# A routed expert loop: the gather with the selection as stationary operand, reading x in place

## The reference, cut to what matters

```
xn = rms_norm(x, norm2_g)                       # 384 x 1024
lg = xn @ rg_w + rg_b ; le = xn @ re_w + re_b   # 4 groups, 32 experts
grp = argmax(lg) ; two best experts in the group, softmax weights -> combine
for e in range(32):
    hdn = silu(xn @ w_gate[e]) * (xn @ w_up[e])   # 1024 -> 512, twice
    out = out + combine[:, e] * (hdn @ w_down[e]) # 512 -> 1024
x = x + out
```

## Time and profile before

| | |
|---|---|
| runs | 946.94, 952.38, 952.4 us |
| the profiled execution's own time | 949.38 us |
| its span, first to last instruction | 947.6 us |
| mean granted TensorE clock | 0.949 |
| TensorE busy | 820.5 us (87%) |
| VectorE, ScalarE, GpSimd busy | 432.2, 312.7, 269.2 us |
| bytes moved | 249.96 MB, mean 264 GB/s |
| first item's gate and up begin | 399.25 us |
| last item's Silu begins | 927.88 us |

### The profile page before, as it was taken

How to read it: one execution, slowest core, us unless ns; L and a number is a source line. 1 busy time by engine, 2 the same in 40 slices (tenths; PEclk the granted TensorE clock), 3 DMA queues, 4 the chain that set the end, 5 groups by cost and what they waited for, 6 DMA issues and landing times.

```text
span 947.6 us, 25723 instructions
## 1 busy us (share of the span) xinstructions
PE 820.5 (87%) x10726; PEld 659.0 (70%) x10727; DVE 432.2 (46%) x1128; ACT 312.7 (33%) x526; POOL 269.2 (28%) x135
## 2 busy tenths in 40 slices
PE   4999999999999999598887767868898889889884
PEld 4999999999999987366555544545666556566663
DVE  3076797899840614533233313223333333334343
ACT  5333875543377226522111111111221112122123
POOL 4755899884858851200000000000000000000000
PEclk9999999999999998799899999889999999999997
DMA  7724334254333326557999999999877999997601
GB/s 242 225 96 133 115 109 152 102 158 145 119 131 118 104 75 257 232 239 285 421 423 423 422 421 423 422 423 422 367 302 313 423 422 422 421 423 292 266 0 67
DMA packets 53170, 249.96 MB, mean 264 GB/s; under 512 B 6599, under 2 KB 6599, under 8 KB 28561
## 3 DMA queue, kind: packets, MB, share of 16 engines
q1 hardware_dynamic: 49184, 244.86, 65.4%
q10 hardware_dynamic: 3953, 4.67, 1.6%
HBM read 246.76 MB, written 2.75 MB: 263 GB/s over the span
## 4 chain that ended last, share of the span: by engine, by line
PE 51%; DVE 22%; DMA 15%; issue 7%; ACT 3%; DVEq 1%; POOL 0%; SPq 0%
PE bank L1240 22%; PE bank L1381 16%; DMA ring<-in_exp_w_up 14%; DVE bank L932 6%; PE bank L1333 4%; PE bank L1238 3%; PE bank L1367 3%; DVE cva L1131 2%; DVE back_to L1159 2%; DVE cva L1155 2%; DVE cvb L1095 1%; DVE y_lo L1168 1%; DMA raw<-in_w_in 1%; DVE ua L994 1%; DVE cvb L1099 1%
## 5 line engine op out<-in xcount | busy, mean ns | idle before, releaser
L1381 PE MATMUL bank<-ring,cvb 128*32 128x256 f32 x2816 | 194.1, 433 | 87.3 <-issue 43.6
L1381 PEld LDWEIGHTS bank<-ring,cvb 128*32 128x32 f32 x2816 | 117.5, 123 | 146.8 <-issue 118.5
L504 POOL TENSOR_TENSOR w_lo<-raw,w_hi 128x2048 fp32r<-128x2048 f32 x40 | 184.9, 4625 | 75.1 <-ACT w_hi L631 75.1
L1149 DVE SCALAR_TENSOR_TENSOR cvb<-bank,slot_coef,cvb 64x256 f32<-64x256 f32 x44 | 21.5, 489 | 289.5 <-ACT cvb L817 289.5
L1240 PE MATMUL bank<-x_hi,w_hi 128*128 128x384 f32 x448 | 150.8, 337 | 0.9 <-POOL w_lo L504 0.6
L1240 PE MATMUL bank<-x_hi,w_lo 128*128 128x384 f32 x448 | 149.7, 334 | 0.0
L1240 PE MATMUL bank<-x_lo,w_hi 128*128 128x384 f32 x448 | 149.7, 334 | 0.0
L932 DVE SCALAR_TENSOR_TENSOR bank<-ub,vec,bank 128x256 f32<-128x256 f32 (+1 forms) x416 | 137.3, 421 | 0.0
L1333 PEld LDWEIGHTS bank<-cvb,ua 128*128 128x128 bf16 x2184 | 79.8, 96 | 50.5 <-issue 38.6
L631 ACT ACTIVATE w_hi<-raw 128x2048 fp32r<-128x2048 f32 x40 | 76.7, 1919 | 83.5 <-PE bank L1240 71.2
L817 ACT ACTIVATE cvb<-bank 64x256 f32<-64x256 f32 x44 | 16.6, 376 | 249.3 <-PE bank L1381 249.3
(11 more groups left out here) (205 smaller groups left out, 1003.5 us busy)
## 6 DMA issues: line engine op xcount, KB each, us to landing
ring<-in_exp_w_gate SPq DMA_DIRECT2D x64, 1024.0 KB, 14.9
ring<-in_exp_w_up SPq DMA_DIRECT2D x64, 1024.0 KB, 16.9
ring<-in_exp_w_down SPq DMA_DIRECT2D x64, 1024.0 KB, 17.9
raw<-in_w_in SPq DMA_DIRECT2D x28, 1024.0 KB, 5.2
raw<-in_w_out_a SPq DMA_DIRECT2D x4, 1024.0 KB, 5.1
raw<-in_w_out_b SPq DMA_DIRECT2D x4, 1024.0 KB, 5.0
raw<-in_w_o SPq DMA_DIRECT2D x4, 1024.0 KB, 5.0
out<-n_tok ACTq DMA_DIRECT2D x3, 512.0 KB, 2.7
```

The costliest lines, as they stand in the source:

```text
L504: pool.tensor_tensor(w_lo[u % NW][:, :, :], raw[u % NW][:, :, :], w_hi[u % NW][:, :, :].bitcast(F32), ALU.subtract).then_inc(lo_ready, 1)
L1149: dve.scalar_tensor_tensor(hid, GU[2 * T:4 * T, :], slot_coef[2 * T:4 * T, 0:1], sig, ALU.mult, ALU.mult)\
L1381: last = pe.matmul(GU[q * T:(q + 1) * T, :], xe[:, k, :], wide(slots[q // 2])[:, k, q % 2 * QE:(q % 2 + 1) * QE], start=(k == 0), stop=(k ...
```

## The change

The gather turns round: `pick` (128 x 32, fp32) is stationary and x moves, 256 columns at a time, read from `x_tok` in place with a step of four floats between columns, so that the rows come out in the order of `by_row`. Four column groups of the array take four different quarters of the row, three token tiles are summed: 12 fp32 matmuls for an item, into `G` (32 slots x 4 blocks on the partitions, 256 columns) in bank 0. ScalarE copies `G` to `rows_of_x`, TensorE transposes it in two pieces into `XT` (the other half of bank 0), and VectorE scales that by `norm2_by_row` into `xe`. The rows are not normalised: the factor of each token (`rstd2`) goes into the slots' coefficients, and the Silu takes it as its scale.

The normalised copies, their three parts and the diagonals are gone, with ScalarE's, GpSimd's and VectorE's work for them. The slot numbers, factors and coefficients are transposed once (`values`, `turned`) and spread by matmuls whose stationary operand is a column of the identity repeated. `Y` lies in bank 0, gate and up in bank 1. The second turn of `combine` comes behind the transposes, the third between the two halves of down; the wait for `y_ready` stands before the gather, the wait for the next `xe` before down. The bounds of a pair's items come by one load of three numbers, and the table holds 33 numbers for 65.

```diff
-    for a, b in zip(range(aux("pos"), len(AUX)), (0, 1, 2, 3, 2, 3)):
+    for a, b in zip(range(aux("pos"), len(AUX)), (0, 1, 1, 2, 1, 2, 1, 2)):
...
-        XE = bank[0][:, 0:KB * T]
+        G = bank[0][:, 0:QE]
+        XT = bank[0][:, QE:2 * QE]
+        Y = bank[0][:, 0:QE]
+        GU = bank[1][:, 0:QE]
         HT = bank[1][:, 0:HK * T]
-        Y = bank[1][:, 0:QE]
-        GU = bank[1][:, 0:QE]
...
             pool.memset(back_to[:].bitcast(F32), 0.0).then_inc(back_ready, 1)
-
-            for i in range(NT):
-                pool.wait_ge(part_ready[0], i + 1)
-                pool.wait_ge(normed, NT + i + 1)
-                pool.tensor_tensor(n_tok[:, i, :], n_tok[:, i, :], parts[0][:, i, :], ALU.subtract)\
-                    .then_inc(rest_ready, 1)
-            for i in range(NT - 1):
-                pool.wait_ge(part_ready[1], i + 1)
-                pool.tensor_tensor(parts[2][:, i, :], n_tok[:, i, :], parts[1][:, i, :], ALU.subtract)\
-                    .then_inc(part_ready[2], 1)
...
-            act.wait_ge(rstd_ready, 1)
-            for i in range(NT):
-                for dst, done in ((n_tok, normed), (parts[0], part_ready[0])):
-                    act.activation(dst[:, i, :].rearrange("p (h j q) -> p h j q", h=2, j=RJ), by_row(x_tok[:, i, :]),
-                                   ACT.Copy, scale=small[:, 32 + i:33 + i]).then_inc(done, 1)
...
+            def copy_rows(n):
+
+                act.wait_ge(gathered, n)
+                act.activation(rows_of_x[:, :], G, ACT.Copy).then_inc(rows_ready, 1)
...
             def item(i):
                 act.wait_ge(gate_up_done, i + 1)
 
-                act.activation(sig, GU[0:2 * T, :], ACT.Silu).then_inc(sig_ready, 1)
+                act.wait_ge(slot_coef_ready, i + 1)
+                act.activation(sig, GU[0:2 * T, :], ACT.Silu, scale=slot_coef[0:2 * T, 0:1]).then_inc(sig_ready, 1)
+                copy_rows(i + 2)
...
             def take_gathered(n):
 
-                dve.wait_ge(gathered, n)
-                dve.tensor_tensor(xe, XE.rearrange("p (k t) -> p k t", k=KB),
-                                  norm2_by_row[:, :].unsqueeze(2).to_broadcast([P, KB, T]), ALU.mult)\
-                   .then_inc(xe_ready, 1)
+                dve.wait_ge(x_turned, n)
+                dve.tensor_tensor(xe[:, :, :].rearrange("p (q b) t -> p q b t", b=2),
+                                  XT.rearrange("p (b q t) -> p q b t", b=2, q=TILES),
+                                  norm2_by_row[:, :].rearrange("p (q b) -> p q b", b=2).unsqueeze(3)
+                                  .to_broadcast([P, TILES, 2, T]), ALU.mult).then_inc(xe_ready, 1)
...
-            def gather(blocks):
-
-                for k in blocks:
-                    for c in range(3):
-                        for i in range(NT):
-                            last = pe.matmul(XE[:, k * T:(k + 1) * T], parts[c][:, i, k * P:(k + 1) * P],
-                                             pick[:, i, :], start=(c == 0 and i == 0), stop=(c == 2 and i == NT - 1))
-                if KB - 1 in blocks:
-                    last.then_inc(gathered, 1)
+            def rows_in_blocks(i, q):
+
+                x = x_tok[:, i, q // 2 * HALF:(q // 2 + 1) * HALF].rearrange("p (n j) -> p j n", j=RJ)
+                return x[:, q % 2 * 2:q % 2 * 2 + 2, :]
+
+            def gather():
+
+                for i in range(NT):
+                    for q in range(TILES):
+                        last = pe.matmul(G[q * T:(q + 1) * T, :], pick[:, i, :], rows_in_blocks(i, q),
+                                         start=(i == 0), stop=(i == NT - 1))
+                last.then_inc(gathered, 1)
+
+            def turn_rows():
+
+                for c in range(2):
+                    last = pe.transpose(XT[:, c * P:(c + 1) * P], rows_of_x[:, c * P:(c + 1) * P], ident[:, :])
+                last.then_inc(x_turned, 1)
...
             def item(i, slots, filled):
 
                 pe.wait_ge(xe_ready, i + 1)
-                pe.wait_ge(y_ready, i + 2)
-
...
-                gather([LATE, LATE + 1])
+                pe.wait_ge(picked, i + 2)
+                pe.wait_ge(y_ready, i + 2)
+                gather()
                 pe.wait_ge(back_ready, i + 1)
                 pe.wait_ge(combined, i * NT + 1)
                 combine(0)
-                gather([LATE + 2])
...
+                pe.wait_ge(rows_ready, i + 2)
+                turn_rows()
                 pe.wait_ge(combined, i * NT + 2)
                 combine(1)
-                pe.wait_ge(hid_ready, i + 1)
-                gather([LATE + 3])
...
-                pe.wait_ge(combined, i * NT + 3)
-                combine(2)
                 pe.wait_ge(hidT_ready, i + 1)
+                pe.wait_ge(xe_ready, i + 2)
                 for part, done in enumerate((down_half, down_done)):
...
                     last.then_inc(done, 1)
-                pe.wait_ge(picked, i + 3)
-                pe.wait_ge(xe_ready, i + 2)
-                gather(range(LATE))
+                    if part == 0:
+                        pe.wait_ge(combined, i * NT + 3)
+                        combine(2)
...
             with pe.Fori(0, NE // 2) as pair:
-                for side in range(2):
-                    e = pair * 2 + side
-                    n = pe.value_load(table[0:1, bass.ds(e, 1)], min_val=1, max_val=N // T)
-                    first = pe.value_load(table[0:1, bass.ds(e + NE, 1)], min_val=0, max_val=MAX_ITEMS - 1)
+                pe.reg_load(bounds, table[0:1, bass.ds(pair * 2, 3)])
...
```

More of the change, by code:

```diff
@@ L97, in trunk_program @@
     AUX += [("pos", 0, "dve"), ("table", 0, "dve")]
-    AUX += [("spread", j, "act") for j in range(4)]
+    AUX += [("turned", 0, "act"), ("spread", 0, "act"), ("spread", 1, "act")]
+    AUX += [("turned", 1, "act"), ("spread", 2, "act"), ("spread", 3, "act")]
     HEAD = 6
@@ L321, in trunk_program @@
         hidT_ready = sem("hidT_ready")
-        part_ready = [sem(f"part{i}_ready") for i in range(3)]
-        rest_ready = sem("rest_ready")
+        rows_ready = sem("rows_ready")
+        x_turned = sem("x_turned")
         sig_ready = sem("sig_ready")
@@ L799, in _ @@
[L799 to L808 removed]
+            act.activation(zero[:, 2:3], zero[:, 0:1], ACT.Exp)
+            act.wait_ge(exp_in, 2)
@@ L1312, in _ @@
                     seed(t, h)
+            seed(0, 1)
             pe.wait_ge(masks_ready, 1)
@@ L1338, in spread, with turn_values, row_of @@
+            def turn_values(j):
+                n = values[j].shape[1]
+                end_aux(pe.transpose(start_aux(aux("turned", j))[0:n, 0:P], values[j], ident[:, :]))
+            def row_of(j, row, n):
+                k = values[j].shape[1]
+                return ident[0:k, row:row + 1].to_broadcast([k, n])
             def spread(j):
-                pe.wait_ge(diagonal_ready, (j + 1) * NT)
                 b = start_aux(aux("spread", j))
-                end_aux(pe.matmul(b[:, 0:N], ones[:, :], diagonal[:, j, :], start=True, stop=True))
+                for i in range(NT):
+                    cols = slice(i * P, (i + 1) * P)
+                    if j < 2:
+                        last = pe.matmul(b[:, cols], row_of(0, j * NT + i, P), turned[0], start=True, stop=True)
+                    else:
+                        pe.matmul(b[0:P // 2, cols], row_of(0, 2 * NT + i, P // 2), turned[0], start=True, stop=True)
+                        last = pe.matmul(b[P // 2:P, cols], row_of(1, (j - 2) * NT + i, P // 2), turned[1],
+                                         start=True, stop=True)
+                end_aux(last)
```

183 lines of the change are left out of this document (90 added, 93 removed).

## The result

The changed kernel takes **942.34 us** (median of 9 runs, 940.46 to 943.70); the kernel before, on the same chip, 949.92 us (9 runs, 946.94 to 953.69). The ratio is 0.9914, with a 95% interval of 0.9893 to 0.9935: 0.9% faster, between 0.7 and 1.1%. The forecast was 913 us. The range of 904 to 950 holds the result, and the first rival, with 940 us, named it almost exactly. The profiled execution took 943.7 us with a span of 941.9.

The account below looks back on a forecast made before the run. Weights' stream (14.89 us an expert) and TensorE (10.03 an item) bind in turn. Request 424.1, + 223.3 = 647.4, + 56.0 = 703.4, stream to 776.3, + 112.8 = 889.1, waits 1.5, end 19.7 + 0.5: span 910.8, forecast 913 us, range 904 to 950.

Parts of the forecast that it names:

- the first rival: Gather's step costs twice, as on ScalarE: gather 2.8 us, item 10.6, kernel 940 us; chance 0.25.
- The gather's price: TensorE's 24 fp32 gather records with a step of four floats: 1.4 us taken, up to 5.5 as the other end.
- The second rival: Column groups share the gather's reads: gather up to 5.5 us, item 13.3, kernel 1010 us; chance 0.12.
- One item: One loop item on TensorE, gate and up through down: 9.2 us for 10.03 before.
- the third rival: ScalarE and VectorE chain outlasts its cover, 0.7 us more before down, or changes of expert stay as costly: about 927; chance 0.13.
- The change of expert: TensorE's cost above an item when the expert changes: 0.4 us on the mean for 2.1, ends 0 and 2.1.
- The start: Routing without GpSimd's work: slots 6.3 us earlier, 10.4 us behind them, first gate and up at 394 for 399.25.
- The walk through the stream: Loop followed from the fourth expert's weight request through weight-stream and TensorE stretches: 18th expert's Silu at 647.4, span 910.8.
- The stream's wait: TensorE's later wait for the weights' stream in the walk with items of 10.6 us: 7 us.
- The end: Stretch from the last Silu to the end of the span: 19.7 us plus 0.5, as down ends later in an item.
- The forecast's own case: Gather of 1.4 us, item of 9.2, kernel 913 us, own range 905 to 928; chance 0.45.
- within 1%: Outcome that the kernel's time changes by no more than 1% either way; chance 0.13.

Follow-up runs that it names:

- the probes: Two kernels: the changed kernel with three single loads of bounds, plus blocks of matmuls read at various steps ahead of the projections; 1025.18 and 1051.91 us.
- copy_one_load: Changed kernel, but ScalarE copies x once into row order and the gather reads that copy without a step, one load of three bounds kept; 916.54 us, ratio 0.9650.
- load_ahead: copy_one_load with the next pair's load of bounds moved behind the gather in the items of a pair's second expert; 915.89 us, ratio 0.9640.
- copy_once: Changed kernel with three single loads of bounds, ScalarE copying x once into row order, the gather reading that copy without a step; 927.84 us, ratio 0.9740.
- pool_beside: copy_one_load with five GpSimd subtractions, whose result nothing uses, put back beside the routing; 923.43 us, ratio 0.9712.

## Why the prediction was wrong

**The gather's price** is the step that failed, as the term "I take 1.4 us" for 24 records: it measures 2.83, the first rival's 2.8. The argument for 1.4 was that float32 leaves half the read rate unused, so that a doubled read would just fit. The kernel with the step of two shows that there is such room (1.46 us), and the probes show how far it goes: float32r pays twice at 8 bytes where float32 pays nothing. At 16 bytes the read costs four times the bare one for bf16, not twice; if float32's read costs the same, its room of two is used up and twice is left. That this is how it comes about is not shown, and float32r, with 0.34 us at 16 bytes, speaks against it. I had taken ScalarE's doubled row as the price of the read, when it was the price of ScalarE's whole operation, and put TensorE's spare rate against it. The row itself, taken as it stands, gives the right answer. The chances should have been the other way round: the only row with this step spoke for twice, against it stood an argument.

**The second rival** (a gather up to 5.5 us for column groups that share reads) is refuted: four groups pay the same factor as one.

**One item**: 10.44 us, of which 2.83 the gather. The other terms sum to 7.6 where the prediction had 7.8, and copy_one_load has the whole at 9.01 for the forecast's 9.2. The wait for xe before down is there, some 0.2 us as in the sum (0.15); the 0.7 of the third rival didn't come.

**The change of expert**: 0.4 us on the mean was taken, with ends 0 and 2.1. Measured: 0.0 inside a pair, 1.33 between pairs, 0.7 on the mean. The granted clock falls less often: it is 0.97 over 657 to 941 us, where the kernel before has 0.94 over 657 to 947. The term was a little small. The sequencer doesn't run ahead over a load at the head of the pair; load_ahead shows that it does so where matmuls are queued. By the three loads a load more costs 0.6 us, and more where the clock falls behind it: in copy_once the idling is 2.44 us long, and gate and up behind it takes 5.35 us for 3.66, the granted clock being 0.68 over 437 to 442 us. With one load it is 1.16 and the clock stays.

**The start**: 394 was taken, 394.86 measured, and the mechanism is shown by pool_beside: GpSimd's work put back costs 7.4 us. VectorE's operations on 96 columns are at 0.26, as said. The slots' numbers are done at 381.7, 6.9 us before 388.58 where the prediction had 6.3. But behind them lie 13.2 us and not the 10.4 of the sum: 2.6 up to the gather, for which 0.9 was put down, and 2.9 for the gather itself instead of 2.1. That the start fits 394 comes from the 1.3 us that were added to the sum's 392.7 without a row.

**The walk through the stream**: held. With the rival's item it gave 652.6 for the 18th expert's Silu and 919.5 for the last; measured 652.33 and 919.54. To the 18th expert that is the mechanism; from there on it is partly luck, as two errors cancel: 24 items of 10.44 and not 10.6 are 3.8 us less, changes of 0.67 and not 0.4 are 3.7 more. The stream's wait was 7 and measures 7.3. The end took 22.4 us for 20.2; 1.4 of that is the step in the last item's gather, which the walk had left out. The rival's 940 is this walk's span, 939.7; with the 1.8 us that the profiled execution takes on top, which the forecast's sum has and the rival's lacks, it is 941.5, against 943.7 of the profiled execution and 942.34 in the median. The forecast's own case was then made real by copy_one_load: 916.54 for 913. Its span is 3.6 us over the walk's 910.8, and 3.0 of that stand already at the 18th expert's Silu (650.44 for 647.4). The first gate and up begins 1.25 us late and takes 5.44 us, the granted clock being 0.66 over it, so that the fourth expert's weights are asked for at 426.21 for 424.1; the stretch of the stream is 0.9 longer. The rest is 0.4 up to the last Silu, where shorter items (9.01 for 9.2) and larger changes nearly cancel, and 0.2 at the end.

**The chances**: the first rival had 0.25 and the forecast 0.45, and 0.9% faster falls into "within 1%", which had 0.13. Both were too low for a case that the only row with this step spoke for.

## What to carry to other kernels

Before a stationary operand is changed so that the moving one is read with a step, price the read: float32 columns 16 bytes apart cost TensorE twice, 8 bytes apart next to nothing, float32r and bf16 pay from 8 bytes on. If the same rows are read again and again, one copy in the right order on an idle engine beats "in place": here 44 gathers at 1.4 us more each against three copies that nobody waits for. And count what an engine's sequencer must fetch where its queue is empty: two loads more at the head of each of 16 pairs took 11 us, and a load behind 24 queued matmuls takes none of TensorE's time. Whether this shortens the kernel is another question: here the weights' stream took it back (915.89 us for 916.54).

## What the runs showed of the hardware

- A matmul's read with a step saturates: at twice in float32 and float32r, at four times in bf16. The first distance of those tried that costs more is 12, 8 and 8 bytes.
- A read of bf16 columns 16 bytes apart keeps its pace when the granted clock falls from 1.00 to 0.50 (0.68 us a record at both), and the clock fell though TensorE had no gap.
- GpSimd's subtraction of two tensors holds up VectorE's operations with two tensors, for 2.06 to 2.45 us in place of 0.26, each up to the end of the subtraction, and lets reductions of one tensor through (0.17, 0.25).
- One load of three numbers into TensorE's registers idles it 1.15 us where nothing is queued, three loads of one number 2.32 us, and a load behind 24 queued matmuls not at all.
